# Packing the on-chip memory map tighter: 32-byte instead of 512-byte rounding, and two small tables moved, in a one-core transformer block

## The reference

```
h    = rmsnorm(x, g_pre_mix);  proj = h @ w_in          # 5192 columns
o_a  = sparse_attention(q_a, k_a, v_a, q_idx, k_idx, w_idx, rel_bias)   # top-128 keys, T5 bias
o_b  = stick_breaking_attention(q_b, k_b, v_b)
m    = sigmoid(gate_a) * (o_a @ w_branch_sparse) + sigmoid(gate_b) * (o_b @ w_branch_sb)
x    = x + rmsnorm(m @ w_out, g_post_mix)
h    = rmsnorm(x, g_pre_ffn);  g, u = split(h @ w_gate_up)
x    = x + rmsnorm((silu(g) * u) @ w_down, g_post_ffn)
```

## Time and profile before

| | |
|---|---|
| runs | 821.0, 815.06, 820.95 us; median 820.95 |
| profiled execution, own time | 821.0 us |
| its span, first to last instruction | 819.3 us |
| mean granted TensorE clock | 0.997 |
| TensorE busy | 793.9 us, 97% of the span |
| mean DMA rate | 94 GB/s, 30.1% of the 16 engines' time |

### The profile page before, as it was taken

The page is one execution under the profiler, slowest core; times in us unless marked ns, Lnnn a source line. Parts: engine busy times, 40 slices in busy tenths (PEclk is TensorE's granted clock), DMA queues, the critical chain, the costliest instruction groups (busy, mean ns, idle before and its releaser), DMA issues.

```text
span 819.3 us, 10762 instructions
## 1 busy us (share of the span) xinstructions
PE 793.9 (97%) x3822; PEld 665.0 (81%) x3822; DVE 387.8 (47%) x539; ACT 326.0 (40%) x472; POOL 405.1 (49%) x246
## 2 busy tenths in 40 slices
PE   6999999999999899999998999999999999999996
PEld 5887888888888788788876988888888888888885
DVE  4359996687786767349707400000000020344464
ACT  5463322656656565543144412222222222322342
POOL 4276464544476867444455134444444444444462
PEclk9999999999999999999999999999999999999999
DMA  7313333223112222223375013333332233232312
GB/s 225 97 52 95 137 116 102 62 59 87 52 54 64 58 59 75 68 78 102 103 253 183 2 53 101 102 102 102 102 102 81 82 93 102 102 102 102 102 52 103
DMA packets 103913, 77.29 MB, mean 94 GB/s; under 512 B 3777, under 2 KB 95945, under 8 KB 103882
## 3 DMA queue, kind: packets, MB, share of 16 engines
q1 hardware_dynamic: 103882, 76.87, 30.1%
HBM read 74.75 MB, written 3.68 MB: 96 GB/s over the span
## 4 chain that ended last, share of the span: by engine, by line
PE 93%; DVE 2%; ACT 2%; issue 1%; DMA 1%; POOL 1%; SPq 0%; ACTq 0%; POOLq 0%; DVEq 0%
PE ps L434 22%; PE ps L406 20%; PE ps L408 20%; PE ps L407 20%; PE ps L627 4%; PE ps L616 2%; PE ps L597 1%; PE ps L595 1%; DMA raw<-in_w_in 1%; DVE x L1377 1%; ACT y_buf L763 1%; PE ps L526 1%; PE ps L468 1%; PE ps L527 1%; DVE y_buf L1182 0%
## 5 line engine op out<-in xcount | busy, mean ns | idle before, releaser
L1043 POOL TENSOR_TENSOR w_lo<-raw,w_hi 128x1024 fp32r<-128x1024 f32 x116 | 281.1, 2424 | 341.3 <-ACT w_hi L737 308.4
L406 PE MATMUL ps<-h_hi,w_hi 128*128 128x512 f32 (+1 forms) x656 | 252.1, 384 | 8.5 <-issue 3.2
L737 ACT ACTIVATE w_hi<-raw 128x1024 fp32r<-128x1024 f32 (+1 forms) x111 | 117.6, 1059 | 334.4 <-PE ps L408 228.1
L408 PE MATMUL ps<-h_hi,w_lo 128*128 128x512 f32 (+1 forms) x656 | 248.9, 379 | 0.0
L407 PE MATMUL ps<-h_lo,w_hi 128*128 128x512 f32 (+1 forms) x656 | 248.8, 379 | 0.0
L406 PEld LDWEIGHTS ps<-h_hi,w_hi 128*128 128x128 f32 x656 | 123.5, 188 | 32.1 <-issue 6.5
L408 PEld LDWEIGHTS ps<-h_hi,w_lo 128*128 128x128 f32 x656 | 123.4, 188 | 23.6
L407 PEld LDWEIGHTS ps<-h_lo,w_hi 128*128 128x128 f32 x656 | 123.6, 188 | 21.4
L1420 DVE TENSOR_TENSOR act<-silu,ps 128x512 f32 (+1 forms) x22 | 15.1, 688 | 211.3 <-PE ps L408 211.3
L1425 DVE TENSOR_TENSOR d_lo<-act,d_hi 128x512 fp32r<-128x512 f32 x18 | 43.1, 2397 | 51.7 <-ACT d_hi L985 51.7
L1052 POOL TENSOR_TENSOR q_lo<-proj,q_twice 64x512 fp32r<-64x512 f32 x16 | 25.5, 1596 | 38.1 <-ACT q_twice L751 37.1
(11 more groups left out here) (179 smaller groups left out, 1221.6 us busy)
## 6 DMA issues: line engine op xcount, KB each, us to landing
raw<-in_w_in SPq DMA_DIRECT2D x44, 512.0 KB, 4.5
raw<-in_w_gate_up SPq DMA_DIRECT2D x44, 512.0 KB, 4.5
raw<-in_w_down SPq DMA_DIRECT2D x22, 512.0 KB, 3.9
raw<-in_w_out SPq DMA_DIRECT2D x8, 512.0 KB, 3.9
x_in<-in_x SPq DMA_DIRECT2D x4, 512.0 KB, 5.6
raw<-in_w_branch_sb SPq DMA_DIRECT2D x8, 256.0 KB, 3.0
raw<-in_w_branch_sparse SPq DMA_DIRECT2D x8, 256.0 KB, 3.0
x<-in_x SPq DMA_DIRECT2D x4, 512.0 KB, 8.0
```

The costliest lines, as they stand in the source:

```text
L406: mm(acc, whi_c, a_hi_, start=first, stop=False)
L408: return mm(acc, wlo_c, a_hi_, start=False, stop=last)
L737: run(w_hi[:, at(u), :], raw[:, at((d % 2) * 2 + u), :], ACT.Copy).then_inc(w_hi_done, 1)
L1043: nc.gpsimd.tensor_tensor(w_lo[:, at(u), :], raw[:, at((d % 2) * 2 + u), :], w_hi[:, at(u), :], sub).then_inc(w_lo_done, 1)
```

## The change

It alters where tensors lie in SBUF, and nothing else.

```diff
-    base = -(-nc.sbuf_base // 512) * 512
+    base = -(-nc.sbuf_base // 32) * 32
...
-    top[0] = zone1 = -(-top[0] // 512) * 512
+    f_bias = sb("f_bias", 384, rows=HEADS)
+    zeros8 = sb("zeros8", 384, rows=HEADS)
+    zone1 = top[0]
...
     tri_f = sb("tri_f", [2, P])
-    f_bias, zeros8 = sb("f_bias", 384, rows=HEADS), sb("zeros8", 384, rows=HEADS)
```

## The result

| | before | changed |
|---|---|---|
| median of 14 runs each | 820.06 us | 824.33 us |
| lowest to highest | 814.92 to 823.65 | 820.97 to 828.64 |
| ratio, 95% interval | | 1.007, 1.0045 to 1.0096 |
| profiled execution, own time | 821.0 us | 822.08 us |
| its span | 819.3 us | 820.3 us |

The changed kernel is slower by 0.7%, 3.7 to 7.9 us by the interval. Both kernels scatter over about 8 us, so one profiled execution of each does not show the loss as a difference of spans (1.0 us); it has to be read from the parts.

What follows compares the result with a forecast made beforehand. It took TensorE, 93% of the span, to bound the kernel. All address terms were 0, leaving the own time at 821.0 us; from the median of three runs, 820.95, it forecast 820.9 us, range 814.5 to 825.

Steps and rivals of the forecast that it cites:

- What bounds the kernel: Whole kernel: TensorE, busy for 793.9 of 819.3 us, so time moves only through matmul spacing or where the chain leaves TensorE.
- the value for matmul operands: TensorE's weights and moving operands at shifted addresses: price taken as zero; 4.1 us bound for 976 matmuls, 16.1 for all.
- the odd `kw` slices: Weight slices 1 and 3 of kw_hi start 32 bytes past a multiple of 64; 0.69 against 0.70 us per three matmuls.
- the 4.2 ns that I took as the largest price: Bound per matmul on placement, of either sign, from two rows of 24 kw matmuls at 231.7 and 227.5 ns each.
- Rival 2: TensorE's moving operands pay up to 4.2 ns off a line: 825 us, or 837; chance 0.05 above 1%, 0.03 below.
- Transfers into `raw`: Weight loads whose 512-byte pieces now land 128 past a multiple of 512: taken as zero, upper end 3.1 us at start.
- The slack of 7 us in the ring: Weight loads in the up projection: a landing could grow from 4.5 to about 12 us before TensorE noticed.
- the estimate of 5.6: Landing time in us for 512-byte pieces by the Trainium skill's page, 20 beats in place of 16, against 4.5 before.
- VectorE, ScalarE and GpSimd operands: Operands of the other engines, in the two norms and the start on the path: price zero, bound under 0.6 us.
- Rival 3: Faster: new residues part engines that met in the same place, between 20 and 400 us; 813 at best; chance 0.07.
- The prediction's last sign: VectorE's and GpSimd's adds in the norm: prediction wrong if placement changes how often engines block each other; no size given.
- rival 1: Transfers get dearer, at the start, stores and norm: 825 us at its upper end, 823 with half; chance 0.09.

Runs made afterwards that it cites:

- the cadence mended: The changed kernel with zones and head on the same remainder modulo 512 and zeros8 left in the zone: 821.50 us, ratio 1.0039.

## Why the prediction was wrong

**What bounds the kernel** was right: the time moved in TensorE's cadence and, by chance of the one execution, in the junction. Attention took 0.8 us more (206.28 and 207.05), within the spread of the fourteen profiles.

**The step that failed** is the value for matmul operands: "The value I take is zero, by the row nearest to the case, the odd `kw` slices." I compared slice 1 with slice 0, found them alike, and concluded that a place 32 bytes off costs nothing. The row was not near to the case. Its weights have 72 columns, and for those no placement gave the 226.7 ns of the 528 matmuls: with every slice at the place of its moving operand they took 233.3. So the 5 ns between 231.7 and 226.7 were no price of placement to be read off either, nor do the 4.2 ns that I took as the largest price bound it: the price was 6.67 ns. And the question was wrong: I asked what an operand's own place costs, when what costs is the distance between weights and moving operand. The whole map moved by 32 bytes costs no cadence (119.69 us); as changed, the two regions apart, the same row costs 3.52 us more. In place of zero this term measured 816 matmuls at 6.67 ns, 5.4 us.

**Rival 2** came nearest, with a wrong mechanism and a wrong count that nearly made up for each other: 976 matmuls at up to 4.2 ns gave 825. Measured were 816. Of the 976, the branch projection's 192 and the 96 of `wd` pay. Attention, which I had counted with 320, has both operands in the zones and pays little: from start to start within its groups of matmuls 46.26 us before and with the whole map moved, 46.67 as changed and with the zones off 32, 0.4 us more. Its 160 transposes stand 109 ns apart both before and as changed. The first tiles of the output and down projections, which I had left out (their moving weights lie in the head), pay on 528. That it says a moving operand off a line pays is refuted by the up projection with its head 32 off.

**Transfers into `raw`**: "I take zero" was wrong for the landings and is open for the time. The landings grew by 0.3 to 0.4 us, not by the half that I allowed at most, and the first transfer did not grow at all (6.15 us on the chain, 6.28 before). The slack of 7 us in the ring did hide them in the loops, as said. (The 6.7 us of the earlier trace rows are two waits, not one; nothing hangs on it.) With the cadence mended a ratio of 1.0039 was left, 0.9 to 5.5 us by its interval, and with `raw` back on a multiple of 512 it was 0.9979; by the two kernels' own medians that is 2.65 us, on two chips. The cadence alone, 5.4 us, already fits the result's interval of 3.7 to 7.9, and the kernel with only its zones moved, where `raw` stays and lands in 4.5 us, lost as much (1.0081). So the result needs no share of the transfers and leaves room for 2.5 us at most. On the destination side the landings thus agree in direction with the rule of the Trainium skill cited in the prediction ("DMA: Bandwidth & Descriptors", "How a descriptor splits into AXI transactions"), which speaks of what is read; in size they do not, 4.9 us against the estimate of 5.6.

**The rest**: VectorE, ScalarE and GpSimd operands show no price at their new places. L1328 (now L1329) has a mean of 1488 ns before and after, ScalarE's roundings 1059 both times, GpSimd's subtractions 2424 and 2430. The stores landed in 2.1 us in place of 2.0. `f_bias` in the head costs nothing that shows; `zeros8` was not tried by itself. Rival 3, faster, did not come: for 512 moving columns every distance tried but 0 and 256 was slower. It was right in one small thing, that a new placement can be faster: the `wu` matmuls gained 1.7 ns each, about 0.1 us in the 48 of the row. The prediction's last sign, adds in the norm that block one another more or less often, did appear (3.03 and 2.88 us before, 1.23 and 1.42 changed), but both the kernel with `raw` back and that with zones off 256 have the long adds again, and no run shows that placement decides it.

**The forecast** of 820.9 us was 3.4 us under the measured 824.33, which lies in the range of 814.5 to 825.0 and within 1% of before. That it lies there is luck: the range was drawn for the scatter of before and for rival 1, not for a dearer matmul. No change was forecast, and the change is clear of noise. The range was wide for the scatter of one kernel, 815 to 821, which a ratio of many runs averages away; that scatter was no reason to expect no difference.

## What to carry to other kernels

A matmul's time can depend on where its two operands lie to each other in SBUF. For the shape that fills this kernel (128-column weights, 512 moving columns, back to back) both at the same remainder modulo 256 bytes was the best of the six distances tried; starting every large tensor on a multiple of 512, as the kernel before does, gives that. Other shapes went another way (256 moving columns, 72-column weights), so compare the start-to-start time of one long row of matmuls for each shape after any change of the memory map; it resolves 0.1 ns, where total times here scatter over about 8 us. Keep destinations of transfers in 512-byte pieces on a multiple of 512 as well: they land 0.3 to 0.5 us sooner, whether or not the kernel waits for them. When a row of before is to price something, take one of the same shape as the operations that the price is for. And when two ratios are compared that were taken at different times, look at the two baselines too.

## What the runs showed of the hardware

- Back-to-back fp32r matmuls with 128-column weights and 512 moving columns took 226.7 ns when weights and moving operand stood at the same place modulo 256 bytes, and 229.0 to 233.3 at the five other distances tried, whatever the place itself. The price is not symmetric: a moving operand 64 bytes further than the weights gave 229.0, one 64 bytes less far 233.3. At these distances the 96 `wd` matmuls (weights in the head) took what the branch projection did, 229.0, and not the 233.3 of the 432 before them, so there it is the direction that counts and not the stage; at 128 the branch projection took 233.3 and `wd` 232.3.
- With 256 moving columns 48 such matmuls took 120.0 ns each at the same place and 116.7 to 118.5 at the others.
- Why the distance counts was not shown. That weight loads and moving reads meet in the memory is a guess; the 72-column weights, at 231.3 to 233.3 ns in all three placements, and the matmuls of 256 columns don't fit a rule by which the same place is always best.
- Loads in pieces of 512 bytes landed in 4.4 to 4.7 us with `raw` on a multiple of 512 and in 4.8 to 5.0 when it stood 32 or 128 past one; loads in pieces of 4096 bytes in 3.8 to 3.9 either way for `w_down`. A multiple of 256 that is none of 512 was not tried for `raw`.
- A VectorE add or product on 128x1024 values took 1.2 to 1.7 us, and 2.9 to 3.5 in cases where it ran beside a subtraction of GpSimd for most of its time. That was not so in every such case, and what decides was not asked.
